# Hybrid decoder layer on one core: two block sums moved to DMAs, and a new order of the operations around the gate product

## The reference

```python
h = h + rms_norm(jnp.einsum('bsf,fd->bsd', ff, w_down[i]), mlp_post_g[i])
gate = jax.nn.sigmoid(jnp.einsum('bsd,de->bse', h, w_ple_gate[i]) + b_ple_gate[i])
ple = jnp.einsum('bsp,pd->bsd', p[i], w_ple[i]) * gate
h = h + rms_norm(ple, ple_post_g[i])
```

## Time and profile before

| | |
|---|---|
| three runs | 582.26, 582.38, 583.83 us |
| profiled execution, its own time | 582.26 us |
| its span in the profile | 580.5 us |
| TensorE busy | 568.4 us, 98% |
| VectorE busy | 504.1 us, 87% |
| ScalarE busy | 375.2 us, 65% |
| GpSimd busy | 111.8 us, 19% |
| granted TensorE clock | 0.994 of full speed over the run |

### The profile page before, as it was taken

The page is one execution under the profiler, slowest core; times in us unless marked ns, Lnnn a source line. Parts: engine busy times, 40 slices in busy tenths (PEclk is TensorE's granted clock), DMA queues, the critical chain, the costliest instruction groups (busy, mean ns, idle before and its releaser), DMA issues.

```text
span 580.5 us, 8931 instructions
## 1 busy us (share of the span) xinstructions
PE 568.4 (98%) x3364; PEld 495.4 (85%) x3364; DVE 504.1 (87%) x643; ACT 375.2 (65%) x595; POOL 111.8 (19%) x161
## 2 busy tenths in 40 slices
PE   9999999999999999999999999999999999999983
PEld 7888888888888888989999998999999999988873
DVE  5789886688766998999989899999999899797996
ACT  6896775775646746667656665575655757676963
POOL 0321546000103463101010011010100100114014
PEclk9999999999999999999999999999999999999997
DMA  8982008224003559478485492774763935889713
GB/s 267 329 331 94 0 2 323 77 72 119 29 1 110 191 199 312 96 215 198 91 255 114 108 280 49 202 197 74 250 150 72 275 89 154 267 251 221 204 49 145
DMA packets 27691, 93.73 MB, mean 161 GB/s; under 512 B 3200, under 2 KB 4608, under 8 KB 27264
## 3 DMA queue, kind: packets, MB, share of 16 engines
q1 hardware_dynamic: 20736, 67.64, 33.2%
q0 software_dynamic: 5328, 19.14, 19.3%
q10 hardware_dynamic: 1584, 6.37, 2.9%
HBM read 86.85 MB, written 6.29 MB: 160 GB/s over the span
## 4 chain that ended last, share of the span: by engine, by line
PE 94%; DVE 2%; POOL 1%; issue 1%; DMA 1%; ACT 0%; DVEq 0%; SPq 0%; POOLq 0%
PE psum L2678 30%; PE psum L2682 29%; PE psum L2683 29%; PE psum L2733 2%; PE psum L2916 2%; PE psum L2896 2%; PE psum L2747 1%; DMA first_raw_a<-weights_dram 1%; DVE acc L1440 0%; POOL stat L2507 0%; DVE w_lo L1352 0%; DVE h L1462 0%; ACT junk_late L1598 0%; PE psum L2770 0%; DVE ple_late_b L1452 0%
## 5 line engine op out<-in xcount | busy, mean ns | idle before, releaser
L2678 PE MATMUL psum<-t_hi,a_hi 128*128 128x512 f32 x216 | 84.7, 392 | 0.0
L2682 PE MATMUL psum<-t_lo,a_hi 128*128 128x512 f32 x216 | 84.6, 392 | 0.0
L2683 PE MATMUL psum<-t_hi,a_lo 128*128 128x512 f32 x216 | 84.0, 389 | 0.0
L2678 PE MATMUL psum<-w_hi,actT_hi 128*128 128x512 f32 (+1 forms) x178 | 69.8, 392 | 1.8 <-DVE acc L1417 1.8
L2683 PE MATMUL psum<-w_hi,actT_lo 128*128 128x512 f32 (+1 forms) x178 | 68.5, 385 | 0.0
L2682 PE MATMUL psum<-w_lo,actT_hi 128*128 128x512 f32 (+1 forms) x178 | 68.4, 385 | 0.0
L2683 PE MATMUL psum<-sum_hi,up_lo 128*128 128x256 f32 x224 | 63.4, 283 | 0.0
L2682 PE MATMUL psum<-sum_lo,up_hi 128*128 128x256 f32 x224 | 63.4, 283 | 0.0
L2678 PE MATMUL psum<-sum_hi,up_hi 128*128 128x256 f32 x224 | 63.2, 282 | 0.0
L2683 PE MATMUL psum<-actT_hi,up_lo 128*128 128x256 f32 (+1 forms) x200 | 60.0, 300 | 0.0
L2682 PE MATMUL psum<-actT_lo,up_hi 128*128 128x256 f32 (+1 forms) x200 | 60.0, 300 | 0.0
(11 more groups left out here) (289 smaller groups left out, 1457.8 us busy)
## 6 DMA issues: line engine op xcount, KB each, us to landing
raw<-weights_dram SPq DMA_DIRECT2D x40, 512.0 KB, 4.9
raw_o<-weights_dram SPq DMA_DIRECT2D x23, 512.0 KB, 4.3
raw_x<-weights_dram POOLq DMA_DIRECT2D x21, 512.0 KB, 5.5
raw_second<-weights_dram SPq DMA_DIRECT2D x16, 512.0 KB, 4.2
raw_x<-weights_dram SPq DMA_DIRECT2D x9, 512.0 KB, 6.0
qk_raw<-weights_dram SPq DMA_DIRECT2D x8, 512.0 KB, 7.5
raw_o<-weights_dram POOLq DMA_DIRECT2D x7, 512.0 KB, 7.2
raw_second<-weights_dram POOLq DMA_DIRECT2D x6, 512.0 KB, 6.9
```

The source lines that it names most:

```text
L2678: begin = nc.tensor.matmul(out, a_hi, b_hi, start=first, stop=False, skip_group_check=read_between)
L2682: nc.tensor.matmul(out, a_hi, b_lo, start=False, stop=False, skip_group_check=read_between)
L2683: return nc.tensor.matmul(out, a_lo, b_hi, start=False, stop=last, skip_group_check=read_between)
```

## The change

- The two sums for OF_S4 (128x512 each) leave VectorE. GpSimd issues them as DMAs that add `gate_s2` to `h2_block(0, 1, j)` inside SBUF (`add_s4`), behind the T4 additions. ScalarE's high part of OF_S4 waits for both DMAs.
- VectorE's order: `gate_ple` 0 and 1, `gain_ple` 0 and 1 and the low part of OF_S4, part 0, go behind `gate_c22(0)`; `gate_ple(6)` goes behind `add_ple(5)`, `gate_ple(8)` behind `add_ple(4)`; `gate_fold(1)`, `gate_c22(1)` and the gains of tiles 2 and 3 change places.
- ScalarE's order: both T4 high parts, OF_S3 part 1 and COPY_E 1 go ahead of `sigmoid(0)`; squares 0 and 1 go behind COPY_CHAIN 1; `sigmoid(3)` ahead of square 2, `sigmoid(6)` ahead of square 5.
- SyncE: `ple_late[0]` is loaded only once T2 part 1 is split, and the gain row is loaded last.
- The last tile: `gate_ple(8)` writes to a buffer of 257 columns, `last_gated`. GpSimd puts the square root of token tile 1's partial sum into its last column (`root_ready`), the last square is taken over all 257 with a scale of 1/32, and so gives the mean directly; the tensor_scalar of the last `ple_rstd` goes.

```diff
--- before.py
+++ after.py
@@ -84,7 +84,7 @@
 GATE_LAST_PART = GATE_P1 + 1
 OF_E, OF_S2, OF_S3, OF_S4 = range(4)
 GATE_SUMS_SPLIT = ((OF_E, 0), (OF_S2, 0), (OF_E, 1), (OF_S3, 0), (OF_S2, 1), (OF_S3, 1), (OF_S4, 0), (OF_S4, 1))
-GATE_SUMS = ((OF_E, 0), (OF_S2, 0), (OF_S3, 0), (OF_S4, 0), (OF_E, 1), (OF_S2, 1), (OF_S3, 1), (OF_S4, 1))
+GATE_SUMS = ((OF_E, 0), (OF_S2, 0), (OF_S3, 0), (OF_E, 1), (OF_S2, 1), (OF_S3, 1))
 COPY_C11, COPY_E, COPY_CHAIN = range(3)
 GATE_COPIES = ((COPY_C11, 0), (COPY_C11, 1), (COPY_E, 0), (COPY_CHAIN, 0), (COPY_E, 1), (COPY_CHAIN, 1))
 
@@ -452,6 +452,7 @@
         ple_gain = place("ple_gain", [P, D], at=at_area + 32 * KIB)
         ple_late = [place("ple_late_a", [P, 2, D], at=at_area + 24 * KIB),
                     place("ple_late_b", [P, 2, D], at=at_mixed_hi)]
+        last_gated = place("last_gated", [P, width_of(LAST_GATED) + 1], at=at_area + 36 * KIB)
         h2T = [place("h2T_a", [P, KD, 2 * P], at=at_area + 16 * KIB),
                place("h2T_b", [P, KD, 2 * P], at=at_mixed_hi + 16 * KIB)]
         gate_e = place("gate_e", [P, 2, 4, P], at=at_mixed_hi + 8 * KIB)
@@ -548,7 +549,7 @@
         c_summed, c_copied = sem("c_summed"), sem("c_copied")
         gate_x_loaded, gate_y_loaded = slab_loaded[0:2], slab_loaded[2:4]
         gate_y_added, late_added = (x_added, o_added), sem("late_added")
-        bias_sum_added, t3_added = 16, 16 + 2 * 16
+        bias_sum_added, t3_added, s4_added = 16, 16 + 2 * 16, 16 + 2 * 16 + 2 * 16
         adds_before = (16 * 3 * LAST, 16 * LAST)
         first_load = 16
         h2_raw, gate_seeded, gate_folded = sem("h2_raw"), sem("gate_seeded"), sem("gate_folded")
@@ -565,6 +566,7 @@
         sig_done, pl_gated, pl_squared, pl_rstd, pl_gained, out_ready = (
             sem("sig_done"), sem("pl_gated"), sem("pl_squared"), sem("pl_rstd"),
             sem("pl_gained"), sem("out_ready"))
+        root_ready = sem("root_ready")
         pool_chain = sem("pool_chain")
 
 
@@ -1395,11 +1397,8 @@
                 elif which == OF_S2:
                     dve.wait_ge(x_summed, gate_sum_at(OF_E, j))
                     first, second, how = gate_e[:, j], a11, ALU.subtract
-                elif which == OF_S3:
+                else:
                     first, second, how = a11, a21, ALU.subtract
-                else:
-                    dve.wait_ge(x_summed, gate_sum_at(OF_S2, j))
-                    first, second, how = h2_block(0, 1, j), gate_s2[:, j], ALU.add
                 nc.vector.tensor_tensor(gate_sum_source(which, j), first, second, how).then_inc(x_summed, 1)
 
             def h2_sum_split_lo(which, j):
@@ -1436,7 +1435,7 @@
                 dve.wait_ge(sig_done, i + 1)
                 if i in (0, 2):
                     dve.wait_ge(ple_loaded[t // 2], 16)
-                gated = acc[:, t, cut]
+                gated = last_gated[:, 0:width] if i == LAST_GATED else acc[:, t, cut]
                 nc.vector.tensor_tensor(gated, acc[:, t, cut], ple_of(t)[:, cut], ALU.mult).then_inc(pl_gated, 1)
 
             GAINED = tuple(range(len(GATE_TILES)))
@@ -1495,7 +1494,6 @@
             h2_sum_split_lo(OF_E, 0)
             gate_split_lo(GATE_T2, 1)
             h2_sum_split_lo(OF_S2, 0)
-            h2_sum(OF_S4, 0)
             gate_split_lo(GATE_T3, 0)
             h2_split_lo(5)
             h2_sum(OF_E, 1)
@@ -1505,41 +1503,40 @@
             gate_split_lo(GATE_T3, 1)
             h2_sum_split_lo(OF_S3, 0)
             h2_sum_split_lo(OF_S2, 1)
-            h2_sum(OF_S4, 1)
-            gate_ple(0)
-            gate_ple(1)
             gate_split_lo(GATE_T4, 0)
-            gain_ple(0)
             gate_split_lo(GATE_T4, 1)
             gate_fold(0)
-            gain_ple(1)
             h2_sum_split_lo(OF_S3, 1)
-            h2_sum_split_lo(OF_S4, 0)
             h2_split_lo(7)
             gate_c22(0)
+            h2_sum_split_lo(OF_S4, 0)
             gate_split_lo(GATE_22, 0)
             gate_split_lo(GATE_22, 1)
             h2_sum_split_lo(OF_S4, 1)
+            gate_ple(0)
+            gate_ple(1)
+            gain_ple(0)
+            gate_fold(1)
             gate_ple(2)
-            gate_fold(1)
+            gain_ple(1)
+            gate_ple(3)
+            gate_c22(1)
             gain_ple(2)
-            gate_ple(3)
             gain_ple(3)
-            gate_c22(1)
             add_ple(2)
             add_ple(3)
             gate_ple(4)
             gain_ple(4)
             gate_ple(5)
             gain_ple(5)
-            gate_ple(6)
             add_ple(0)
             add_ple(5)
+            gate_ple(6)
             gain_ple(6)
             gate_ple(7)
-            gate_ple(8)
             gain_ple(7)
             add_ple(4)
+            gate_ple(8)
             add_ple(6)
             gain_ple(8)
             add_ple(1)
@@ -2171,10 +2168,12 @@
 
             def h2_sum_split_hi(which, j):
 
-                act.wait_ge(x_summed, gate_sum_at(which, j))
                 if which == OF_S4:
+                    act.wait_ge(late_added, s4_added)
                     act.wait_ge(up_filled, gate_at(2, j))
-                elif which == OF_S2:
+                else:
+                    act.wait_ge(x_summed, gate_sum_at(which, j))
+                if which == OF_S2:
                     act.wait_ge(up_filled, gate_at(0, j))
                 elif which == OF_S3:
                     act.wait_ge(up_filled, gate_at(1, j))
@@ -2222,6 +2221,10 @@
             def square_ple(i):
                 t, c0, width = GATE_TILES[i]
                 act.wait_ge(pl_gated, i + 1)
+                if i == LAST_GATED:
+                    act.wait_ge(root_ready, 1)
+                    square(last_gated[:], ss_pl[:, i:i + 1], pl_squared, 1 / ROOT_D)
+                    return
                 square(acc[:, t, c0:c0 + width], ss_pl[:, i:i + 1], pl_squared)
 
             seed_down(4)
@@ -2265,29 +2268,29 @@
             h2_sum_split_hi(OF_S3, 0)
             h2_sum_split_hi(OF_S2, 1)
             gate_copy(COPY_E, 0)
+            gate_split_hi(GATE_T4, 0)
+            gate_copy(COPY_CHAIN, 0)
+            gate_split_hi(GATE_T4, 1)
+            h2_sum_split_hi(OF_S3, 1)
+            gate_copy(COPY_E, 1)
             sigmoid(0)
             sigmoid(1)
-            gate_copy(COPY_CHAIN, 0)
-            gate_split_hi(GATE_T4, 0)
-            gate_split_hi(GATE_T4, 1)
-            h2_sum_split_hi(OF_S3, 1)
             h2_sum_split_hi(OF_S4, 0)
-            square_ple(0)
-            square_ple(1)
-            gate_copy(COPY_E, 1)
             gate_split_hi(GATE_22, 0)
             gate_split_hi(GATE_22, 1)
             h2_sum_split_hi(OF_S4, 1)
             sigmoid(2)
             gate_copy(COPY_CHAIN, 1)
+            square_ple(0)
+            square_ple(1)
+            sigmoid(3)
             square_ple(2)
-            sigmoid(3)
             square_ple(3)
             sigmoid(4)
             sigmoid(5)
             square_ple(4)
+            sigmoid(6)
             square_ple(5)
-            sigmoid(6)
             sigmoid(7)
             square_ple(6)
             sigmoid(8)
@@ -2470,6 +2473,14 @@
                 nc.gpsimd.dma_start(gate_source(block, part), weights[gate_in_stream(pair)], accum_op=ALU.add
                                     ).then_inc(added, 16)
 
+            def add_s4(j):
+
+                if j == 0:
+                    pool.wait_ge(late_added, t3_added)
+                pool.wait_ge(x_lo_done, h2_split_at(2 * j + 1))
+                pool.wait_ge(x_summed, gate_sum_at(OF_S2, j))
+                nc.gpsimd.dma_start(h2_block(0, 1, j), gate_s2[:, j], accum_op=ALU.add).then_inc(late_added, 16)
+
             def down_rstd(t):
                 pool.wait_ge(dn_squared, t + 1)
                 rstd(rstd_dn[:, t:t + 1], ss_dn[:, t:t + 1], D, dn_rstd)
@@ -2489,6 +2500,8 @@
             down_rstd(3)
             add_gate(GATE_T4, 0)
             add_gate(GATE_T4, 1)
+            add_s4(0)
+            add_s4(1)
 
             def partial_sum(i):
 
@@ -2501,10 +2514,14 @@
             def ple_rstd(t):
 
                 last_tile = gate_tiles_of(t)[-1]
+                mean = ple_mean
                 pool.wait_ge(pl_squared, last_tile + 1)
-                after(nc.gpsimd.tensor_scalar(ple_mean, ss_pl[:, last_tile:last_tile + 1], ple_partial[:, t:t + 1],
-                                              1.0 / D, ALU.add, ALU.mult))
-                nc.gpsimd.tensor_tensor(rstd_pl[:, t:t + 1], ple_mean, minus_half[:, 0:1], ALU.pow
+                if last_tile == LAST_GATED:
+                    mean = ss_pl[:, last_tile:last_tile + 1]
+                else:
+                    after(nc.gpsimd.tensor_scalar(mean, ss_pl[:, last_tile:last_tile + 1], ple_partial[:, t:t + 1],
+                                                  1.0 / D, ALU.add, ALU.mult))
+                nc.gpsimd.tensor_tensor(rstd_pl[:, t:t + 1], mean, minus_half[:, 0:1], ALU.pow
                                         ).then_inc(pl_rstd, 1)
```

(5 more changed lines are left out.)

## The result

| | median | runs | profiled execution | its span |
|---|---|---|---|---|
| before | 582.46 us | 4 (582.26 to 583.83) | 582.26 us | 580.5 us |
| after | 590.02 us | 4 (589.15 to 590.49) | 590.04 us | 588.3 us |

The ratio is 1.0122, 95% interval 1.0103 to 1.0143. The forecast was 584.2 us in a range of 581.2 to 587.3: the direction was right, though the prediction gave slower no better chance than same (0.46 each); the size was four times too small, and the time lies outside the range. In the table of experiments one run is left out: e1's fourth took 3242.89 us, for a reason that is not known, where its other three lie between 584.84 and 586.04.

A forecast was written before the change was run, and what follows sets the result against it. TensorE was taken as the bound (94% of the chain that ended last), then VectorE's tail waiting for GpSimd. TensorE's 2.0 us gain would not reach VectorE; the last add_ple moves +1.9 us: 582.26 + 1.9 = 584.2 us, range 581.2 to 587.3.

The forecast's parts named there:

- Up to the stall: TensorE's 1.8 us wait at product (5,0) for VectorE's subtraction goes, as gate_c22(0) starts at 553.4 instead of 556.90 us.
- The OF_S4 additions: Both DMAs, behind T4 part 1, land between 551.9 and 556.5 us, taken as 554.2; product (4,1) starts on time.
- Rival 2: Additions land at 556.5 us or later and product (4,1) waits 2.3 us: 586.4 us, or 587.4 at 557.5; chance 0.22.
- The tail: After the stall VectorE waits for GpSimd's small operations; the last add_ple ends at 579.9 us, +1.9 us.
- rival 3: GpSimd slips between VectorE's operations; partial sum 7 and added power take 0.27 and 0.57: 581.2 us; chance 0.12.
- rival 1: Both additions land by 552 us, T4 part 1 unhindered: +0.8 to +1.2, 583.1 to 583.5 us; chance 0.27.
- The rule for GpSimd: GpSimd operations started during VectorE's tensor_tensor on two SBUF tensors end only after it; 13 operations fit within 0.1 us.
- Rival 4: T4 part 1 lands at 553.0 us, the (5,0) stall stays at 1.8 to 2.1 us: 587 us; chance 0.06.

The follow-up runs named there:

- e1: The kernel after with the two OF_S4 sums back on VectorE at their old places, the rest as changed; 585.25 us, ratio 1.0051.
- e2: The kernel after with the turned h stored so that an OF_S4 block is one 2 KB row per partition instead of four of 512 bytes; 586.18 us, ratio 1.0076.
- e6: The kernel before with only the two OF_S4 sums turned into GpSimd's DMAs, orders and loads as before; 584.13 us, ratio 1.0047.
- e4: The kernel after with the load of ple_late[0] and the gain row back at their old place in SyncE's queue; 586.54 us, ratio 1.0079.
- e3: The kernel after with 68 unused matmuls ahead of product (4,1), to keep TensorE busy while it waits; 589.10 us, ratio 1.0117.
- e7: The kernel after with the OF_S4 sums on VectorE and the last tile as before, without the added power; 584.04 us, ratio 1.0044.
- e5: The kernel before with only another order of VectorE's and ScalarE's operations, laid out by hand; 582.01 us, ratio 0.9999.
- e11: The kernel before with only the change's orders on VectorE and ScalarE; sums, loads and last tile as before; 583.26 us, ratio 1.0010.
- e10: The kernel after with 2 KB rows for the OF_S4 blocks and the loads of ple_late[0] and the gain row early; 583.79 us, ratio 1.0016.
- e12: The kernel before with another written order, ple_late[0] loaded late and the means moved from GpSimd to VectorE; 583.08 us, ratio 1.0013.

## Why the prediction was wrong, point by point

**Up to the stall: right.** The wait for L1417 went. T2 part 1 landed 9.4 us after its issue instead of 11.9, and ScalarE no longer waited for it. `gate_c22(0)` was forecast for 553.4 and came at 555.23; 0.8 of that is the later start of the stretch, the rest is T4 part 1, which took 9.2 us and landed at 551.2, where 549.3 was forecast.

**The OF_S4 additions: the step that failed.** Forecast 554.2, at most 556.5; measured 559.5, or 558.7 with the 0.8 of the later start taken off. Of the 4.5 us too little, 1.1 is T4 part 1 and 3.4 the additions behind it: 8.3 us from the landing of T4 part 1 (551.2) to theirs, where I took 4.9 between bounds of 2.6 and 7.2. Two mistakes are in it. The bounds came from transfers of long rows, and e2, with long rows, has 5.8 us in place of the 8.3, inside my bounds; the short rows are 2.5 of the 3.4. The late loads made no difference to this term in these traces: with the loads early it was still 8.4 and 8.8 us (e6, e4); what they delayed is T4 part 1. And the bounds of the second term were put on the middle of the first: with T4 part 1 at its own upper bound of 553.0 they would have reached 560.2, and the range 590.

**What followed from it: right.** Rival 2 was the mechanism: TensorE waits for ScalarE's copy, and each microsecond later is one more at the end. It had 582.2 for a landing at 556.5; with 558.7 that is 584.4, and 585.2 with the 0.8, against 585.79 measured. The 0.6 left is about what e3's stretch gives for the clock (0.7), which the prediction did not have; that the two are the same is not shown. The share of 0.22 was too low: a transfer of a kind that no row shows, behind a 512 KB addition and beside 1 MB, was put at the middle of its bounds. (For a landing at 557.5 the prediction has 587.4 in one place and 587.3 in another.)

**The tail: right in kind.** Partial sum 7 took 1.10 us (forecast 1.09), the added power 0.92 (1.29), the last root 0.55 (0.57), and the mean that is dropped saves less than they cost (e7). "GpSimd slips between" (rival 3) did not happen. What the tail costs where no addition holds anybody up, e1 shows, which has the two sums on VectorE besides: 1.7 us by the stretch, 3.0 by the ratio; rival 1, without that wait and those sums, had 0.8 to 1.2.

**The rule for GpSimd: partly wrong.** It held for the 13 operations of before and failed in e5, where two of them took 3.10 us together. Which gap lets GpSimd in stays open.

**Rival 4** (T4 part 1 late, the stall stays) had 553.0 for the landing; 551.2 lies midway between that and the forecast's 549.3. Its stall did not come.

**Where the 6.9 us of the stretch went**, step by step along the kernels: orders 0.3 (before to e11), late loads 0.2 (e11 to e7), the added power 1.1 (e7 to e1), the additions 5.2 (e1 to after). Within the last, short rows 3.7 (e2) and the loads beside them 3.1 (e4) overlap. Each number is from one profiled execution. By the ratios the additions are 4.1 us of 7.1 and the late loads 2.0 (1.0010 to 1.0044): both say that the additions are the largest part, and the split of the rest is open.

## What to carry to other kernels

An operation of 0.6 us on an engine that has slack later is poorly exchanged for a DMA whose result is due within 10 us: first find a row with the same kind, the same row length and the same neighbours, and where there is none, add the upper bounds of all the links of the chain before calling the sum a range. Where engines are nearly balanced, a stall taken out of one (1.8 us of TensorE here) comes back as waits between the others (nothing of it was left in e11); look at what ends last before counting the gain.

## What the hardware showed that I had not expected

- **Short rows inside SBUF.** 256 KB added by DMA from SBUF to SBUF took 14.3 and 13.6 us with rows of 512 bytes (after) and 10.8 and 10.6 with rows of 2 KB (e2), both beside 1 MB and 512 KB loads. With `ple_late[0]` early the first addition took about the same with either (8.1 in e4, 8.3 in e10), the second 10.3 and 8.1; there the issue times differ as well. The Trainium skill, "DMA: Bandwidth & Descriptors" (Why small descriptors are slow (HBM only)), says that transfers inside SBUF don't suffer from small descriptors; the pair of after and e2 does not bear that out for additions. The estimate of 2.6 us that the prediction worked out from the same page of the Trainium skill (Anatomy of one DMA) is a third or less of every addition here; none ran without other transfers beside it.
- **TensorE's clock after a wait.** Waits of 1.41 us (e2) and 1.82 us (before) left the granted clock at 1.00; waits of 2.00 us (e4) and 4.37 us (after) were followed by some 3 and 5 us at 0.50. In e6 a wait of 2.10 us left it at 1.00 (matmuls of 0.39 us), so the length of the wait alone does not decide.
- **GpSimd beside VectorE.** An operation on 128x1 numbers that takes 0.27 us beside an idle VectorE took up to 1.70, and in e12 a power of 0.57 took 1.49 and ended only with VectorE idle.
